# The head sums of a decoder block as rounded one-pass products, and the inverse norm on GpSimd

## The reference

```
kk = (k * k_k).reshape(B, T, H, N)
kk = kk / jnp.maximum(jnp.linalg.norm(kk, axis=-1, keepdims=True), 1e-12)
k = k * (1.0 + (a - 1.0) * k_a)
...
bonus = jnp.sum(rh * kh * r_k, axis=-1, keepdims=True) * vh
```

## Time and profile before

| | |
|---|---|
| median of 3 runs | 1890.52 us (1889.84 to 1890.83) |
| the profiled execution, its own time | 1889.0 us |
| the span of its profile | 1887.2 us |
| TensorE busy (matmul) | 1857.9 us, 98% |
| VectorE busy | 1173.3 us, 62% |
| ScalarE busy | 771.8 us, 41% |
| GpSimd busy | 457.2 us, 24% |
| mean granted TensorE clock | 0.996 |

### The profile page before, as it was taken

One profiled execution on the slowest core, in us unless ns is written; L12 is line 12 of the kernel. 1 busy time (PEld: TensorE's weight loads), 2 busy tenths in 40 slices (PEclk: granted clock), 3 DMA queues, 4 the chain that ended last, 5 costly groups with the idle time before them and its releaser, 6 DMA issues.

```text
span 1887.2 us, 38317 instructions
## 1 busy us (share of the span) xinstructions
PE 1857.9 (98%) x15168; PEld 1509.3 (80%) x15168; DVE 1173.3 (62%) x2238; ACT 771.8 (41%) x1545; POOL 457.2 (24%) x1096
## 2 busy tenths in 40 slices
PE   8999999999999999999999999999999999999996
PEld 5878888888888887888888888888888778888885
DVE  4666575766767577666766667676767754356433
ACT  6434444443434344444443434343435443243221
POOL 0005051423324150051423324150505051101110
PEclk9999999999999999999999999999999999999998
DMA  5433332323332335332333233333333543365433
GB/s 180 164 109 99 89 93 83 94 89 93 89 92 88 90 94 171 111 88 84 93 89 94 88 89 90 92 94 88 91 85 101 164 133 102 128 206 168 156 127 125
DMA packets 194962, 207.70 MB, mean 110 GB/s; under 512 B 98272, under 2 KB 101472, under 8 KB 194784
## 3 DMA queue, kind: packets, MB, share of 16 engines
q1 hardware_dynamic: 194784, 205.26, 36.5%
HBM read 183.18 MB, written 22.02 MB: 109 GB/s over the span
## 4 chain that ended last, share of the span: by engine, by line
PE 95%; DVE 3%; ACT 1%; DMA 1%; issue 0%; DVEq 0%; SPq 0%; ACTq 0%
PE psum L1153 77%; PE psum L1138 3%; PE psum L1289 2%; PE psum L1224 2%; PE psum L1262 1%; PE psum L1442 1%; PE psum L1406 1%; PE psum L1323 1%; PE psum L1208 1%; PE psum L1249 1%; PE psum L1413 1%; PE psum L1179 1%; PE psum L1162 1%; PE psum L1194 1%; PE psum L1395 1%; PE psum L1332 0%
## 5 line engine op out<-in xcount | busy, mean ns | idle before, releaser
L1153 PE MATMUL psum<-x_hi,w_hi 128*128 128x512 f32 x2144 | 882.2, 411 | 9.3 <-DVE x_lo L741 7.5
L1153 PE MATMUL psum<-x_hi,w_lo 128*128 128x512 f32 x2144 | 837.6, 391 | 0.0
L1153 PE MATMUL psum<-x_lo,w_hi 128*128 128x512 f32 x2144 | 837.4, 391 | 0.0
L732 DVE TENSOR_TENSOR w_lo<-w_raw,w_hi 128x512 fp32r<-128x512 f32 x536 | 378.5, 707 | 588.9 <-ACT w_hi L539 569.0
L539 ACT ACTIVATE w_hi<-w_raw 128x512 fp32r<-128x512 f32 x536 | 335.4, 629 | 793.3 <-PE psum L1153 772.0
L1153 PEld LDWEIGHTS psum<-x_hi,w_hi 128*128 128x128 f32 x2144 | 403.3, 188 | 111.6 <-DVE w_lo L732 17.4
L1153 PEld LDWEIGHTS psum<-x_hi,w_lo 128*128 128x128 f32 x2144 | 402.7, 188 | 88.6
L1153 PEld LDWEIGHTS psum<-x_lo,w_hi 128*128 128x128 f32 x2144 | 404.0, 188 | 79.9 <-issue 7.2
L495 POOL TENSOR_TENSOR sub_t<-sub_l,sub_io 128x60 f32<-128x60 f32 (+24 forms) x496 | 187.9, 379 | 893.5 <-DMA sub_l<-scratch_L 855.9
L497 POOL TENSOR_TENSOR sub_io<-sub_io,sub_t 128x60 f32<-128x60 f32 (+24 forms) x496 | 192.9, 389 | 38.9
L516 POOL TENSOR_TENSOR v<-v,kb 128x512 f32<-128x512 f32 x29 | 38.5, 1326 | 269.1 <-ACT kb L678 268.9
(11 more groups left out here) (236 smaller groups left out, 1797.3 us busy)
## 6 DMA issues: line engine op xcount, KB each, us to landing
w_raw<-in_w_in SPq DMA_DIRECT2D x408, 256.0 KB, 2.6
w_raw<-in_w_out SPq DMA_DIRECT2D x128, 256.0 KB, 2.6
sub_l<-scratch_L SPq DMA_DIRECT2D x16, 512.0 KB, 4.5
stage<-in_x_t SPq DMA_DIRECT2D x20, 256.0 KB, 3.4
stage<-scratch_MIX SPq DMA_DIRECT2D x19, 256.0 KB, 3.7
scratch_MIX<-sa SPq DMA_DIRECT2D x16, 256.0 KB, 3.3
scratch_MIX<-ym SPq DMA_DIRECT2D x16, 256.0 KB, 3.2
lora<-in_x_t SPq DMA_DIRECT2D x16, 256.0 KB, 2.8
```

Source lines behind the costliest of these rows:

```text
L732: nc.vector.tensor_tensor(w_lo[gq % SPLIT][:], w_raw[gq % RAW][:], w_hi[gq % SPLIT][:].bitcast(F32), ALU.subtract).then_inc(w_ready, 1)
L1153: mm = nc.tensor.matmul(psum[:, s % 2], wt[gq % SPLIT][:, cols], xx[:, c], start=(c == 0 and wt is w_hi and xx is x_hi), stop=(c == KC - 1 ...
```

## The change

The head sums are made by the same rounded one-pass products as the projection. For each of the two sums the squares (or the bonus products) are split into a high and a low part, and two matmuls of 512 columns with `heads_r`, the 0/1 matrix in the rounded type, add both parts. Channels stay on the partitions, so there is nothing to transpose and the sum is already spread over the head's channels. The inverse of the 128x512 sums is made by GpSimd: a power with exponent -1, then a Newton step (multiply, multiply-add by constants, multiply), and GpSimd also multiplies `k` by it. Several steps change their numbers: `turn_p(i, 1)` from 13 to 14, `shift(v)` from 14 to 15, the shift of `r` from 21 to 20, the bonus products from 22 to 21, the gate product `sa` from 21 to 22, and the making of `qr` from 13 to 18 (16 in the last interval of a half). The second half's norm loads go to `late` in place of `wr`, `kkt` and `zs`. At the start the load of `par1` moves behind the first weights and the first input chunk, and ScalarE does a tiny copy ahead of its first wait, and the wait for `par1` comes after the first weights.

```diff
+        heads_r = sb("heads_r", [P, P], F32R)
-        eps = sb("eps", [P, 2])
+        eps = sb("eps", [P, 3])
...
+        kkt, kkt_r = with_rounded("kkt", [P, BH, C])
+        zs, zs_r = with_rounded("zs", [P, BH, C])
+        wr, wr_r = with_rounded("wr", [P, BH, C])
...
-        second = [z[:].rearrange("p m d -> p (m d)") for z in (wr, kkt, zs)]
+        second = [late[:, i] for i in range(SECOND)]
...
                     if ph == 1 or ph == 2:
-                        sp.wait_ge(kk_read, PAIRS * ph)
+                        sp.wait_ge(divided, PAIRS * ph)
...
+                load_w(0)
+                load_x(0, 0)
                 sp.dma_start(par1[:], io["par1"]).then_inc(par1_landed, 16)
-                load_w(0)
-                for c in range(2):
-                    load_x(0, c)
+                load_x(0, 1)
                 sp.dma_start(cst[:], io["consts"]).then_inc(consts_landed, 16)
...
+                        if j < INTERVALS and at == 15:
+                            pool.wait_ge(inv_ready, j + 1)
+                            power = eps[:, 2:3].broadcast_to([P, HALF])
+                            inv, rest = sub_l_f[:, 0:HALF], sub_l_f[:, HALF:]
+                            then(nc.gpsimd.tensor_tensor(inv, grow, power, ALU.pow))
+                            then(nc.gpsimd.tensor_tensor(rest, grow, inv, ALU.mult))
+                            then(nc.gpsimd.tensor_scalar(rest, rest, -1.0, 2.0, ALU.mult, ALU.add))
+                            then(nc.gpsimd.tensor_tensor(inv, inv, rest, ALU.mult))
+                            then(nc.gpsimd.tensor_tensor(grow, k, inv, ALU.mult))
+                            pool.sem_inc(divided, 1)
...
                     if at == 5:
                         act.wait_ge(k_ready, j + 1)
-                        nc.scalar.activation(s1, k, ACT.Square, scale=p(n, "k_k")).then_inc(squares, 1)
+                        if j >= 2:
+                            act.wait_ge(u_full, 2 * (j - 1))
+                        nc.scalar.activation(s1, k, ACT.Square, scale=p(n, "k_k"))
+                        nc.scalar.activation(kkt_r[:], k, ACT.Square, scale=p(n, "k_k")).then_inc(squares, 1)
+                    if at == 22:
+                        act.wait_ge(rkr_ready, j + 1)
+                        copy(zs_r[:], s1).then_inc(rkr_high, 1)
...
                     if at == 11:
                         act.wait_ge(kkt_full, i + 1)
+                        if i < INTERVALS - 1:
+                            act.wait_ge(norm_done, i + 2)
...
-                    if at == 13:
+                    if at == 14:
                         turned_p(i, 1)
...
                         act.wait_ge(y_centred, i + 1)
+                        if i < INTERVALS - 1:
+                            act.wait_ge(bonus_done, i + 2)
...
                 act.wait_ge(inited, 1)
-                act.wait_ge(par1_landed, 16)
+                copy(part[:, 0:3], eps[:])
                 for part_ in range(4):
                     high(part_)
+                    if part_ == 0:
+                        act.wait_ge(par1_landed, 16)
...
-                    if at == 14:
+                    if at == 15:
                         shift(v[:], p(n, "mu_v"))
...
-                    if at == 11:
-                        dve.wait_ge(norm_done, 2 * j + 1)
-                        then(nc.vector.tensor_scalar(inv2[:], psum[:, 2, 0:BH], 1e-24, None, ALU.max))
-                        then(nc.vector.reciprocal(inv2[:], inv2[:]))
-                        then(nc.vector.tensor_copy(grow.rearrange("p (m d) -> p m d", d=HD),
-                                                   inv2[:].unsqueeze(2).broadcast_to([P, BH, HD])))
+                    if at == 6:
+                        dve.wait_ge(squares, j + 1)
+                        then(nc.vector.tensor_tensor(wr_r[:], s1, kkt_r[:].bitcast(F32), ALU.subtract))
+                        dve.sem_inc(squares_split, 1)
+                    if at == 14:
+                        dve.wait_ge(norm_done, j + 1)
+                        then(nc.vector.tensor_scalar(grow, psum[:, 3], 1e-24, None, ALU.max))
                         dve.sem_inc(inv_ready, 1)
-                    if at == 13:
-                        dve.wait_ge(norm_done, 2 * j + 2)
-                        then(nc.vector.scalar_tensor_tensor(k, k, p(n, "k_k"), psum[:, 3], ALU.mult, ALU.mult))
-                        dve.sem_inc(kk_read, 1)
+                    if at == (16 if last_of_half(j) else 18):
+                        dve.wait_ge(divided, j + 1)
+                        dve.wait_ge(kkt_full, j)
                         for c in range(2):
-                            ins = nc.vector.tensor_tensor(
-                                qr[:, :, 2 - c], k.rearrange(chunks, b=NB, c=2)[:, :, c],
-                                decay[:, :, 0:C].rearrange("p (b c) t -> p b c t", c=2)[:, :, c], ALU.mult)
+                            ins = nc.vector.scalar_tensor_tensor(
+                                qr[:, :, 2 - c], grow.rearrange(chunks, b=NB, c=2)[:, :, c], p(n, "k_k"),
+                                decay[:, :, 0:C].rearrange("p (b c) t -> p b c t", c=2)[:, :, c], ALU.mult, ALU.mult)
                         then(ins)
...
-                    if at == (25 if last_of_half(j) else 21):
+                    if at == (25 if last_of_half(j) else 22):
...
-                    if at == (17 if last_of_half(j) else 21):
+                    if at == (17 if last_of_half(j) else 20):
                         shift(r, p(n, "mu_r"))
+                    if at == 23:
+                        dve.wait_ge(rkr_high, j + 1)
+                        then(nc.vector.tensor_tensor(kkt_r[:], s1, zs_r[:].bitcast(F32), ALU.subtract))
+                        dve.sem_inc(rkr_split, 1)
...
-                    if at == 22:
+                    if at == 21:
...
+                nc.vector.tensor_copy(heads_r[:], const("same_head"))
...
-                    if at == 10:
-                        pe.wait_ge(squares, j + 1)
-                        pe.wait_ge(sigma_w, j + 1)
-                        if j >= 2:
-                            pe.wait_ge(yt_read, j - 1)
-                        for b in range(NB):
-                            mm = nc.tensor.matmul(psum[:, 2, 2 * b:2 * b + 2], s1[:, b * P:(b + 1) * P],
-                                                  const("head_of"), start=True, stop=True)
-                        mm.then_inc(norm_done, 1)
-                    if at == 12:
-                        pe.wait_ge(inv_ready, j + 1)
+                    if at == 9:
+                        pe.wait_ge(squares_split, j + 1)
                         pe.wait_ge(sigma_a, j + 1)
+                        pe.wait_ge(z_read, j)
                         if j % PAIRS == 0:
                             pe.wait_ge(va_read, j // PAIRS + 1)
-                        for b in range(NB):
-                            mm = turn(psum[:, 3, b * P:(b + 1) * P], grow[:, b * P:(b + 1) * P])
-                        mm.then_inc(norm_done, 1)
+                        nc.tensor.matmul(psum[:, 3], heads_r[:], kkt_r[:], start=True, stop=False)
+                        nc.tensor.matmul(psum[:, 3], heads_r[:], wr_r[:], start=False, stop=True
+                                         ).then_inc(norm_done, 1)
                     if at == 24:
-                        pe.wait_ge(rkr_ready, j + 1)
-                        pe.wait_ge(kk_read, j + 1)
-                        nc.tensor.matmul(psum[:, 3], const("same_head"), s1, start=True, stop=True
+                        pe.wait_ge(rkr_split, j + 1)
+                        pe.wait_ge(inv_ready, j + 1)
+                        nc.tensor.matmul(psum[:, 3], heads_r[:], zs_r[:], start=True, stop=False)
+                        nc.tensor.matmul(psum[:, 3], heads_r[:], kkt_r[:], start=False, stop=True
                                          ).then_inc(bonus_done, 1)
...
-                    if at == 13:
+                    if at == 14:
                         turn_p(i, 1)
```

More of the change, by code:

```diff
@@ L74 @@
 for _name, _w in (("ident", 128), ("same_head", 128), ("mean", 128), ("amask", 256), ("dist", 192),
-                  ("dist0", 192), ("head_of", 2)):
+                  ("dist0", 192)):
     CONSTS[_name] = (_at, _at + _w)
@@ L93, in constants @@
     t["dist0"] = np.where((d >= 0) & (d < BT) & (key + r - r % SB >= BT), d, 1e33)
-    t["head_of"] = (r // HD == np.arange(2)[None, :])
     return np.concatenate([t[n].astype(np.float32) for n in CONSTS], axis=1)
@@ L163, in sb, with with_rounded @@
             return ctx.enter_context(nc.sbuf_tensor(name, shape, dt))
+        def with_rounded(name, shape):
+            offset = nc.sbuf_base
+            return sb(name, shape), nc.alloc_sbuf_tensor_at(name + "_r", [P, HALF], F32R, offset=offset)
         def sem(name):
@@ L186, in program @@
         lora_up = [sb(f"lora_up{i}", [P, P]) for i in range(2)]
-        inv2 = sb("inv2", [P, BH])
+        heads_r = sb("heads_r", [P, P], F32R)
```

(19 more changed lines are left out.)

## The result

The kernel after takes 3015.57 us (median of 4 runs, 3014.96 to 3017.15); the kernel before took 1890.67 us beside it (4 runs). The ratio is 1.595, 95% interval 1.593 to 1.597. The profiled execution took 3015.81 us, its span is 3013.9 us.

A forecast was written before the change was run, and what follows sets the result against it. TensorE's own list was taken as the bound: 1889.0 - 21.3 (list) - 0.5 (start) + 9.0 (late `level(i, 0)`) = 1876.2, or 1877.7 as a median, stated as 1877 us; range 1866 to 1922, 8 in 10.

The forecast's parts named there:

- I take 1.3, the row of the same instruction form on the same engine, and keep 6.3 for the range.: GpSimd's power over 512 columns: 1.3 us like its product, 6.3 us from VectorE's reciprocal as the estimate from above.
- The second rival: A long power holds the shared port, TensorE waits at `corner(i)` for `level(i, 0)`: 15 x (X - 2.0), 1933 at X = 6.3; chance 0.28.
- X: The time of GpSimd's power in one interval, taken as 1.3 us.
- A wait there would begin to cost only when X passes some 14 us.: VectorE's wait at 18 for GpSimd's result, ahead of `transition`: 7 us to spare, no cost until X passes some 14 us.
- there a long X costs about as much as in the next paragraph: Two intervals where VectorE asks at 16, `level(i, 1)` behind the wait: a long X costs about the port conflict's X - 2.0.
- 21.3 us: TensorE's list: 2.24 us an interval lost, 0.91 gained, so 1.33 saved, times 16; 18.1 with the upper bound.
- The price of the pair: Four rounded matmuls of 512 columns an interval, at 9 and 24, cost the stream's 0.2275 us each, 0.91 in all.
- `turn_p(i, 1)` moves from 13 to 14 and costs the same there: TensorE's `turn_p(i, 1)`, moved from 13 to 14: no change in cost.
- each microsecond taken from TensorE's own list shortens the kernel by one, as long as no other engine becomes late: TensorE, busy 88.59 of 88.60 us an interval: time saved on its list shortens the kernel equally unless another engine becomes late.
- The shape of the conflict at 15 and 16: VectorE and GpSimd alternate at the shared port, making `level(i, 0)` 0.6 us late in 15 intervals: 9 us.
- No wait at all: Rival: the power is short, `level(i, 0)` keeps its 1.4 us of spare time, and the kernel takes 1868.7 us; chance 0.27.
- The 0.5: The gain at the start from the new order of loads and the earlier table load: between 0 and 1.7 us, taken as 0.5.

The follow-up runs named there:

- the cheap operation: The changed kernel with GpSimd's power replaced by a product by a column of zeros, leaving out the inverse: 1894.27 us, ratio 1.0021 to the kernel before.
- blocks and corner moved: The changed kernel with VectorE's reciprocal for power and Newton step, `under(i)` and `corner(i)` each behind the first six matmuls of their quarters (16, 17): 1875.88 us, ratio 0.9917.
- the kernel before with the power aside: The kernel before with an unused GpSimd power of 256 columns added at 15 in each interval: 1891.9 us, ratio 1.0002.
- the blocks moved alone: The changed kernel with VectorE's reciprocal for power and Newton step, only `under(i)` moved behind the first six matmuls of quarter 16: 1890.04 us, ratio 0.9993.

## Why the prediction was wrong

**The failed step: "I take 1.3, the row of the same instruction form on the same engine, and keep 6.3 for the range."** The power took 81.93 us, 63 times the product of the same form. Neither end held it: the lower came from the form, the upper from VectorE's reciprocal, an operation of another engine. The choice of the same form as the nearest row was the mistake; a power shares with a product how it is written, and the runs show that its time is of another size. The prediction itself said that no row showed a power, and then let the two bounds carry a chance of 8 in 10. The page "GPSIMD Engine Reference" of the Trainium skill (section "Performance pitfalls for Q7 kernels"), quoted there for a chain of dependent steps, spoke for a longer time; it gives none for this operation, and no run here shows whether the power is such a chain.

**The second rival, "the power is long and holds the port".** The first half was so, the second not. Beside a power of 41 us VectorE's weight split takes 0.69. The power of the kernel after that begins at 568.75 and takes 81.94 (in the chain above) leaves the splits at 0.69 too, and so do all 60 splits that lie within its powers:

```profile
570.58 0.69 DVE L760 TENSOR_TENSOR w_lo<-w_raw,w_hi 128x512 fp32r<-128x512 f32 x1 [1.97 <-ACT w_hi L555]
```

The rule "SBUF: two separate sides" of the page "SBUF — State Buffer" of the Trainium skill, by which the lock is held for a whole instruction, fits GpSimd's products (1.79 for 0.69) and not its power. So it is luck that this rival's price, 15 x (X - 2.0), comes near with the measured X (1868.7 + 15 x 79.9 = 3067, measured 3015.6): it has TensorE stand at 17 for `level(i, 0)`, and TensorE stood at 20, behind the wait of VectorE at 18.

**"A wait there would begin to cost only when X passes some 14 us."** This was right in its place and nearly in its size: the wait came at 18 in VectorE's list, `transition` was behind it, TensorE stopped at 20, and the cover was 15 to 16 us. By the prediction's own numbers it is 15.5 (the five operations end at 453.4 + X, and VectorE's three pieces of 3.25 us must begin by 468.94); 14.2 is what X may grow by beyond its 1.3. With X = 81.93 put in, that gives a wait of 66.4, and the trace has 65.8 in the mean. An interval is 68.2 us longer (156.9 for 88.7), the wait and the slower matmuls less what the list saves. Only the price was missing. For the intervals 7 and 15, where VectorE asks at 16, "there a long X costs about as much as in the next paragraph" (X - 2.0, 79.9) was near: 78 us each.

**TensorE's list, "21.3 us".** The list lost 19.0 us by busy time with the cheap operation and 22.8 with blocks and corner moved; in that kernel an interval that nothing disturbs is 1.54 us shorter (88.68 and 87.14), where 1.33 was costed. The price of the pair was right where it stands in front of the stream:

```profile
548.63 0.66 PE psum L1173 x6
549.29 0.23 PE psum L1229
549.52 0.23 PE psum L1230
549.75 5.44 PE psum L1188 x24
```

At 24 the first matmul of the pair comes behind small tiles and takes 0.43, the second 0.24.

```profile
673.33 0.43 PE psum L1235
673.75 0.24 PE psum L1236
673.99 2.77 PE psum L1188 x12
```

That is 0.67 for the pair in place of 0.455, but the quarter behind it takes 2.77 and not the 2.94 that stands behind small tiles: 3.44 together, 3.40 by the prediction's terms. "`turn_p(i, 1)` moves from 13 to 14 and costs the same there" was not so: its six transposes take 0.87 at 13 in the kernel before and 0.66 at 14 in the kernel with blocks and corner moved, and this 0.2 is what the costed saving of 1.33 lacks:

```profile
443.58 0.87 PE psum L1138 x6
...
439.99 0.66 PE psum L1168 x6
```

**The step that would have failed next: "each microsecond taken from TensorE's own list shortens the kernel by one, as long as no other engine becomes late".** I looked for lateness at the places that the edit touches, and something became late elsewhere: without the power the whole saving went into the return of the blocks at 16, 1.15 us in the mean interval, and `level(i, 0)` at 17. A wait that ends in time is in no list of waits, but the trace of the kernel before has the two times: the last return landed 1.5 us before `under(i)` in the interval shown above, and 0.4 to 2.6 us before it in the sixteen. Set beside a list that is to lose 1.33 us an interval, this would have shown the limit in advance. The shape of the conflict at 15 and 16 was right (five operations in a row, `level(i, 0)` about 0.6 late, 0.6 in the mean of the times it was waited for), but this was seven times and not fifteen, 4.1 us and not 9.0, TensorE being late at 16 already, and it was not the largest wait. "No wait at all", 1868.7, was reached by no kernel; the best is 7 us above it. In the kernel with blocks and corner moved 6.5 us stand in a wait for VectorE (L776), 3.0 and 2.8 of them in the intervals 7 and 15, where the tiles come in another order.

**The start.** The third piece of the stream in the chain begins at 12.56, and at 13.76 before, 1.2 us. But single profiles do not fix so small a number: the kernel before with the power aside, whose start is untouched, has this piece at 13.11, and the kernels with the new start have it at 11.69 to 13.47. The 0.5 stands inside that.

**What stays open.** How GpSimd makes a power, and so whether other values than those tried take the same time. Why the block path takes some 0.8 us more with the cheap operation than before (44.6 and 43.8) was not taken apart. Whether the blocks could be loaded earlier, which would free the saving without moving `under` and `corner`, was not tried.

## What to carry to other kernels

An operation that no trace shows on that engine has no bound from rows of other operations: measure it alone before it goes onto a path, or make the case that it does not decide. Where one engine is the bound, ask before shortening its list what runs past it with a length of its own (a DMA out and back, an inversion on a side engine), and how much spare time each of its waits has (the landing or end of what it waits for, set beside the start of the reader); the saving ends where the first of these binds. And when a wait is removed by moving its reader, move the reader of that reader in the same step: with the blocks moved alone the kernel only came level with the kernel before.

## What the runs showed of the hardware that was not expected

- A power of 128x512 values on GpSimd takes 81.93 us and one of 128x256 takes 41.12 to 41.15, 160 ns a column, against 2.5 ns a column for a product. Exponent 1 on zeros and ones took as long as exponent -1 on sums of squares.
- While it runs, VectorE's operations with two inputs keep their time (0.69), which beside a GpSimd product they do not (1.79).
- After a stall of 66 us the granted clock of TensorE was 0.50 of full in the next 7.6 us, and twelve matmuls of the stream took 2.67 + 1.84 us where they take 2.9 at the full clock: 1.6 us behind that stall, beside the stall itself.
